# The 24 units of dilated attention between the dense matmuls of two runs, four steps a slot, a unit's weights turned one step behind its scores

## What is computed

```python
h = rms_norm(x, norm_w); proj = h @ w_in            # split into a_u, a_v, a_z, b_q, b_k, b_v, b_z, m_q, m_z, g
q = rms_norm(b_q per head, b_q_norm_w); k = rms_norm(b_k per head, b_k_norm_w); v = b_v    # 12 heads of 64
for gi, (window, dilation) in enumerate(((128, 1), (512, 4), (2048, 16))):                  # 4 heads each
    scores = q_block @ k_blocks.T / 8 + bias          # causal, window // dilation steps back
    m = max(scores); p = exp(scores - m); l = sum(p); o = p @ v / l; lse = m + log(l)
wts = softmax(stack(lses)); y_b = sum(wts * o) * silu(b_z)
# y_a: gelu(a_u), gelu(a_v), spatial gating, silu(a_z);  y_m: attention to 256 memory tokens, silu(m_z)
merged = sigmoid(g0) * (y_a @ proj_a) + sigmoid(g1) * (y_b @ proj_b) + sigmoid(g2) * (y_m @ proj_m)
x = x + merged @ w_out                                # second_block follows, untouched
```

## Time and profile before

| | us |
|---|---|
| median of 2 runs | 1762.23 (1761.26 to 1763.2) |
| span of the profiled execution | 1759.4 |
| PE busy / weight loads busy | 1726.5 / 1398.6 |
| DVE / ACT / POOL busy | 914.9 / 654.1 / 249.0 |
| the stretch of dilated attention alone (262.7 to 326.4) | 63.7 |
| PE / DVE / ACT busy in it | 60.2 / 53.6 / 56.0 |
| granted TensorE clock in it | 0.97 of full speed |

### The profile page before, as it was taken

How to read it: one execution, slowest core, us unless ns; L and a number is a source line. 1 busy time by engine, 2 the same in 40 slices (tenths; PEclk the granted TensorE clock), 3 DMA queues, 4 the chain that set the end, 5 groups by cost and what they waited for, 6 DMA issues and landing times.

```text
span 1759.4 us, 22322 instructions
## 1 busy us (share of the span) xinstructions
PE 1726.5 (98%) x8731; PEld 1398.6 (79%) x8731; DVE 914.9 (52%) x1528; ACT 654.1 (37%) x1225; POOL 249.0 (14%) x412
## 2 busy tenths in 40 slices
PE   7999999999999999999999999999999999999998
PEld 5788887778888888778888788888887777777786
DVE  5158868664336744763222322467242545657764
ACT  5234438611324432752112211233313363434731
POOL 3012210188801100000000000482000000000000
PEclk9999999999999999999999999999999999999999
DMA  4121110346232200311111221242713111001132
GB/s 145 52 76 47 37 37 2 118 144 192 85 123 72 61 25 13 94 30 49 54 42 52 66 63 31 96 144 79 156 31 99 42 31 37 25 25 48 40 130 107
DMA packets 148339, 122.93 MB, mean 70 GB/s; under 512 B 10555, under 2 KB 133898, under 8 KB 147594
## 3 DMA queue, kind: packets, MB, share of 16 engines
q1 hardware_dynamic: 148234, 121.49, 22.9%
HBM read 108.21 MB, written 13.26 MB: 69 GB/s over the span
## 4 chain that ended last, share of the span: by engine, by line
PE 56%; DVE 2%; ACT 1%; issue 1%; DVEq 0%; ACTq 0%
PE psum L93 30%; PE psum L278 10%; PE psum L81 7%; PE psum L2707 2%; PE psum L2738 2%; PE psum L2721 1%; PE psum L1720 1%; PE psum L945 0%; PE psum L931 0%; PE psum L2503 0%; PE psum L2524 0%; PE psum L920 0%; PE psum L2217 0%; DVE ya_low L1572 0%; PE psum L1481 0%
## 5 line engine op out<-in xcount | busy, mean ns | idle before, releaser
L93 PE MATMUL psum<-hT,w_parts 128*128 128x512 f32 x3360 | 796.4, 393 | 7.1 <-PEq L61 3.4
L93 PEld LDWEIGHTS psum<-hT,w_parts 128*128 128x128 f32 x3360 | 629.3, 189 | 144.7 <-issue 8.9
L221 DVE TENSOR_TENSOR w_parts<-w_raw,w_parts 128x1024 fp32r<-128x1024 f32 x88 | 111.7, 1270 | 364.9 <-ACT w_parts L210 364.9
L93 PE MATMUL psum<-h2T,w_parts 128*128 128x512 f32 x1248 | 297.1, 394 | 0.0
L93 PEld LDWEIGHTS psum<-h2T,w_parts 128*128 128x128 f32 x1248 | 230.8, 188 | 48.3 <-issue 1.7
L1514 ACT ACTIVATE gate<-psum,cols 128x512 f32<-128x512 f32 x48 | 33.1, 689 | 284.1 <-PE psum L81 284.0
L81 PE MATMUL psum<-y_high,wp_parts 128*128 128x512 f32 x384 | 128.8, 395 | 0.3 <-DVE ya_low L1572 0.3
L210 ACT CAST w_parts<-w_raw 128x1024 fp32r<-128x1024 f32 x88 | 91.6, 1041 | 24.7 <-DMA w_raw<-w_in 19.5
L81 PEld LDWEIGHTS psum<-y_high,wp_parts 128*128 128x128 f32 x384 | 72.0, 188 | 18.9 <-DVE ya_low L1572 1.6
L278 PE MATMUL psum<-w_parts,y_parts 128*128 128x512 f32 x360 | 82.6, 390 | 0.6 <-DVE w_parts L271 0.6
L403 DVE RECIPROCAL x<-x 128x512 f32<-128x512 f32 x24 | 80.2, 3341 | 0.0
(11 more groups left out here) (377 smaller groups left out, 2298.5 us busy)
## 6 DMA issues: line engine op xcount, KB each, us to landing
w_raw<-w_in SPq DMA_DIRECT2D x188, 256.0 KB, 3.4
middle_a<-ada_w SPq DMA_DIRECT2D x32, 384.0 KB, 3.7
w_raw<-w_out SPq DMA_DIRECT2D x16, 512.0 KB, 3.8
qkT<-x SPq DMA_DIRECT2D x8, 512.0 KB, 7.9
w_raw<-m_w_kv SPq DMA_DIRECT2D x16, 256.0 KB, 3.1
base<-x SPq DMA_DIRECT2D x8, 512.0 KB, 4.0
x_kept<-x_ring SPq DMA_DIRECT2D x8, 512.0 KB, 3.8
base<-x_kept SPq DMA_DIRECT2D x8, 512.0 KB, 3.6
```

What stands on the lines that cost most here:

```text
L93: last = pe.matmul(out, lhs(a, k), rhs(b, k), start=(n == 0), stop=(n == len(SLOT) - 1))
L221: dve.tensor_tensor(self.parts[:, u, LO, :, :], self.raw[:, :, :], self.parts[:, u, HI, :, :].bitcast(F32), ALU.subtract).then_inc(self.lo ...
```

## The change

In words: the 24 units are cut into 26 *bodies*. Body b does, on PE, scores of unit b, the turn of unit b-1 and the mix of unit b-2 (`lag=1`); on ACT the copy of unit b-1 and the exponentials of unit b; on DVE the store of unit b-3, the maxima of unit b and the copy of unit b-1. A slot has four places for a body, on PE behind 6, 12, 18 and 24 dense matmuls. Bodies 0 to 14 stand in slots 36 to 39 of the first run (body 0 at slot 36's second place), bodies 15 to 25 in slots 0 to 2 of the middle run. On ACT and DVE the first three places are written at the slot's start and the fourth at its end: on ACT behind the slot's eviction and the rounding of weights, on DVE behind the weights' low part and `vector_last`.

Dense matmuls keep two banks (0, 1) in these slots, so one score buffer is left (banks 2-3), one `pT`, and the weights lie in three places. The middle run's tile 0 is rounded in slot 37 (`ahead_high`, `ahead_low` at the last-but-one tile instead of at the run's end; this holds for the middle run's end too). Join starts two slots later (`FIRST = 3`) and spreads both pairs of a group in one slot (slots 5, 6, 7); Modulation starts in slot 4, the SSM loads in slot 3, MemNorm in slot 21, with its steps 3 slots apart and not 4. One more normal tile stands ahead of the memory's small tiles, and the last two of these follow each other.

```diff
@@ Dense.tensor
-            slot_part(pe, out, lhs, rhs, range(8))
+            slot_part(pe, out, lhs, rhs, range(6))
+            for work in self.beside:
+                work.tensor_body(pe, s, 0)
+            slot_part(pe, out, lhs, rhs, range(6, 8))
...
                 work.tensor_mid(pe, s)
+                work.tensor_body(pe, s, 1)
...
                 before.after(pe, self, s - 1)
+            for work in self.beside:
+                work.tensor_body(pe, s, 2)
             last = slot_part(pe, out, lhs, rhs, range(18, 24))
@@ Dense.scalar
+            for place in range(3):
+                for work in self.beside:
+                    work.scalar_body(act, s, place)
...
             if slot.last and slot.n + 2 < len(self.tiles):
                 w.split_high(act, slot.n // 2 + 1, slot.n % 2)
+            elif slot.last and slot.n + 2 == len(self.tiles) and self.ahead:
+                self.ahead.ahead_high(act)
             for work in self.beside:
                 work.scalar(act, s)
+                work.scalar_body(act, s, 3)
...
-        if self.ahead:
-            self.ahead.ahead_high(act)
@@ Dense.vector
+            for place in range(3):
+                for work in self.beside:
+                    work.vector_body(dve, s, place)
...
+            elif slot.last and slot.n + 2 == len(self.tiles) and self.ahead:
+                self.ahead.ahead_low(dve)
             self.tiles[slot.n].vector(dve, self, s)
             if s:
                 self.tiles[self.slots[s - 1].n].vector_last(dve, self, s - 1)
             for work in self.beside:
                 work.vector(dve, s)
+                work.vector_body(dve, s, 3)
@@ Attention.scores
             pe.wait_ge(self.maxed, u - before + 1)
-            pe.wait_ge(self.exped, u - before + 1)
+            if self.units[u - before]["bias"] is None:
+                pe.wait_ge(self.exped, u - before + 1)
@@ Attention.maxima
+        if u >= 2:
+            dve.wait_ge(self.exped, u - 1)
@@ DilatedAttention
-        super().__init__(core, stack, units, ident, p, pT, (0, 2), 4, (6, 7), lag=2)
+        super().__init__(core, stack, units, ident, p[0], pT, (2,), 4, (6, 7), lag=1)
+    def body_pe(self, pe, b):
+        lag = self.lag
+        if b < self.n:
...
+            self.scores(pe, b)
+        if 0 <= b - lag < self.n:
+            if b == lag:
+                pe.wait_ge(self.before.rooted, len(self.before.heads))
+            self.turn(pe, b - lag)
+        if b - lag - 1 >= 0:
...
+            self.mix(pe, b - lag - 1)
+    def body_act(self, act, b):
+        if 0 <= b - self.lag < self.n:
+            self.move_act(act, b - self.lag)
+        if b < self.n:
+            self.exps(act, b)
+    def body_dve(self, dve, b):
...
+        if 0 <= b - self.lag - 2:
+            self.store(dve, b - self.lag - 2)
+        if b < self.n:
+            self.maxima(dve, b)
+        if 0 <= b - self.lag < self.n:
+            self.move_dve(dve, b - self.lag)
@@ Join.tensor
-        if 2 <= s < 8:
-            g, pair = (s - 2) // 2, s % 2
+        if 2 <= s < 5:
+            g = s - 2
...
+            for pair in range(2):
+                if g:
+                    pe.wait_ge(self.used, 2 * g + pair - 1)
@@ first_block
+            last_slots = run.first_slot(len(values + queries + keys))
+            first_bodies = DilatedBodies(dilated, 0, 4 * last_slots + 1)
+            run.beside.append(first_bodies)
+            last_bodies = DilatedBodies(dilated, first_bodies.body(len(run.slots) - 1, 3) + 1, 0, after_last=True)
```

More of the change, by code:

```diff
@@ L517, in scalar @@
             work.scalar_start(act)
-        if self.heads:
+        if self.heads and not self.same_at:
             act.copy(self.same, self.same_from).then_inc(self.same_made, 1)
@@ L890, in __init__, with place @@
                 "stored"))
+    def place(self, u):
+        return self.p[u % self.ring]
     def S_(self, u):
```

239 lines of the change are left out of this document (127 added, 112 removed).

## The result

| | before | after |
|---|---|---|
| median, first measurement | 1762.23 (2 runs) | 1788.4 (2 runs) |
| ratio with its 95% interval | | 1.0154 [1.0138, 1.0171] |
| median, second measurement | 1762.16 (10 runs) | 1788.12 (4 runs, 1785.7 to 1790.2) |
| ratio with its 95% interval | | 1.0143 [1.0128, 1.0159] |
| span of the profiled execution | 1759.4 | 1786.7 |

A forecast was written before the change was run, and what follows sets the result against it. PE, busy 1726.5 of 1759.4 us, was taken as the bound. Fill -5.6, switches +6.0, waits +26.3, clock +3.2, Join and rest -1.8 gave +28.1: span 1787.5, median 1790 us, range 1766 to 1804.

The forecast's parts named there:

- Switches: Going from dense matmuls to a unit and back on PE costs 0.23 us, 26 bodies: +6.0 us.
- The stretch's fill and drain go: Filling and draining of the dedicated dilated attention stretch, lowered clock included, disappears: -5.6 us.
- Waits: New PE waits for a unit's scores or turn between dense matmuls, four kinds: +26.3 us.
- (a): Slot 36: the heads' reciprocals on DVE stand ahead of the first units' maxima, delaying scores and turns: 7.4 us.
- (b): Slot 37, the runs' border, middle run's slot 1: maxima wait behind a tile's rounding and low part: 12.3 us.
- (c): Slots 38, 39 and middle run's slot 0: Exp's table load after Silu's delays the turn: 4.4 us.
- (d): Copy of one unit waits for the mix before it through one `pT`, in seven wide bodies: 2.2 us.
- The clock: Two falls of the clock behind PE's waits, 1.65 us each: +3.2 us.
- Join and the rest: Join's spreading matmuls -1.35, middle run's end -0.8, small tiles' wait 1.0; together -1.8 us.
- Not slower: Rival: DVE's and ACT's order does not bind, dense matmuls cover the chain; 1754 to 1765 us, chance 0.09.
- Half hidden: Rival: PE's waits absorb the switches, and DVE and ACT run ahead; 1765 to 1777 us, chance 0.13.
- The waits stack: Rival: each delayed step delays those behind it, with four clock falls; over 1797.5 us, chance 0.18.

The follow-up runs named there:

- all_off: Changed kernel with one head tile's reciprocal cut to 64 columns, fourth body ahead of rounding and low part, Copy for Silu at eight pieces, lag of two: 1765.3 us.
- order3: Changed kernel with the fourth body's exponentials and maxima ahead of the weights' rounding and low part in a tile's last slots: 1786.5 us.
- all_but_order: Changed kernel with reciprocal cut to 64 columns, Copy for Silu and lag of two, but its own order on ACT and DVE: 1765.1 us.
- best: Kernel before with units 0 and 1 started in slots 37 and 38, Join's two pairs in one slot, next run's first weights rounded earlier: 1757.8 us.
- after_again: The changed kernel once more with no edit: 1788.12 us.
- recip_cut: Changed kernel with the reciprocal of one head tile's roots taking 64 columns instead of 512 in slots 34 and 35: 1784.8 us.
- order_tables: Changed kernel with the fourth body ahead of rounding and low part, and Copy for Silu in the gates and the middle run's first two tiles: 1782.7 us.
- no_tables: Changed kernel with Copy instead of Silu for the first run's gates and the middle run's first two tiles: 1778.6 us.

## Why the prediction was right, and where it was not

**Switches: right.** Six dense matmuls between two bodies of after take 1.59 us where nothing waits (335.47 to 337.06 on PE's timeline), against 1.36 for six of a long row: 0.23, the value of the earlier trace rows. all_off agrees with the sum. The Trainium skill (TensorEngine Tiling (Array Packing), Key Properties) has TensorE drain at a change of the tiling mode; the trace agrees in so far as a visit costs that 0.23 us.

**The stretch's fill and drain go: in line with the runs, and it is all there was to win.** With every new cause off, the changed kernel still stands 4.1 us over the kernel before: the switches cost what the fill gave, and some waits remain.

**Waits: right in their places, too large in sum.** Forecast were 26.3 of waits, 3.2 of clock and -5.6 of fill, 23.9 together; the rows give 16.5 and at most 8.2, 24.7. From start to start, with the time from a release to the matmul, the units of after lose 21.2 us by waits, 5 less than forecast.

- (a) The reciprocals: 7.4 forecast; 3.82, 0.34, 0.41 and 0.99 at slot 36 are 5.6, or 5.9 from start to start. Taken away alone it gave 3.3, put back alone it cost 5.5. The cause is shown, and with it that ACT's roots and table load are the next to be waited for.
- (b) Maxima behind a tile's weights: 12.3 forecast at three places; there the rows have 9.5 (2.39, 0.97; 1.01, 1.39; 2.74, 0.96), or 9.9 from start to start. Places and chain were right, and the rows of DVE at 278.32 show it. What did not hold is that the order of rounding, low part and maxima is the cause by itself: turning it round should bring back the 7.1 us at slot 37 and slot 1, and neither order3 (waits 19.6 of 19.7) nor all_but_order (1765.1 against 1765.3) shows any worth of it. The unit is late at a slot's end because a table load, eviction, rounding and low part, or else eviction, copy and two table loads, stand between a slot's last matmul and a turn one body later. The two chains are of nearly one length.
- (c) Tables: 4.4 forecast as waits of their own; 1.03, 1.04 and 1.56 at 304.06, 322.07 and 342.75 are 3.6, one behind each of the slots named. The size was right, but it is not what the loads cost: taking 14 of them away gave 9.6, for Silu's load also delays the rounding and so the maxima of (b), and with shorter waits four of five lengths of low clock went. The Trainium skill (ScalarE: Activation LUTs, What ACT_TABLE_LOAD costs) adds a drain to a load; in order3's rows the exponential follows the load of 280.30 within 0.02 us of its end, and here as in the earlier trace rows no drain shows (there the first exponential starts at 264.72).
- (d) One `pT`: 2.2 forecast, the four waits of 0.25 and 0.26 before turns, 1.0 together. Not tried by itself, since a second buffer has no room.

**The clock: mis-sized, and the step that failed.** Two falls of 1.65 were forecast for 3.2. The units of after have five lengths of 3.4 us low; where PE works in them it loses 6.7 us from start to start (1.2, 1.6, 1.5 and, behind the double one, 2.4), and at the middle run's end the fall doubled (+1.2): 7.9. The prediction took the number of falls from the one in the stretch of before; the changed kernel waits 3.8 us, 2.4 and 1.0, 1.0 and 1.4, 2.7 and 1.0, and has a fall behind each of the four. That the total came out nearly exact is luck: waits 5 us too large and clock 4.7 us too small cancel.

**Join and the rest: in line, not measured alone.** 27.3 at the end, 25.2 at L1837, 26.9 behind the small tiles, 26.1 at the middle run's end: the wait of the small tiles was 1.42 (1.0 forecast), the gain at the end 0.8 as forecast. Behind slot 3 the shift grows by no more than 2.1 us. The -1.35 for Join's matmuls was not taken apart in the changed kernel; in best, with the weights rounded earlier, it is part of 3.9.

**The rivals.** "Not slower" turned on the reciprocals and the order on DVE; all_off, which takes the reciprocals, the order, the tables and the short lag away, lands at 1765.3, the upper edge of it (1754 to 1765); the order alone decided nothing. "Half hidden" did not happen: switches and waits add. "The waits stack" needed four falls and half of the waits more; there were four low stretches, one of them double, and fewer waits than forecast. ACT and DVE are only 63% and 55% busy from 243 to 365 us, and in most bodies between the slots' ends PE waits 0.26 us at most.

## What to carry to other kernels

Before units are put between dense matmuls, ask what the stretch they come from wastes: here 5.6 us, a price that 26 changes of the matmuls' form eat by themselves. Then follow the unit through the slot's end, not the order of two instructions: eviction, rounding, table loads and reciprocals make a chain, and with a turn one step behind its scores each link counts; removing one link of two equally long chains buys nothing. No change of table inside the mixed slots (9.6 us) and a lag of two (5.0) gave more than the reordering (1.6). And where PE is 97% busy, a wait costs its length and, in this kernel, often some 1.5 us of clock behind it.

## What the runs showed of the hardware

The time at the low clock came in portions of about 3.4 us (now and then 6.8): 3.4, 3.4, 3.4 and 6.8 in the units of after, the same in after_again, and none in all_off. A portion cost 1.2 to 1.7 us where PE was busy. In after, falls stand behind waits of 3.8, 2.4 and 2.7 us and behind two of 1.01 and 1.39 us that follow each other, in the kernel before behind 1.82; none behind the single waits of 1.03, 1.04 and 1.56 at 304.06, 322.07 and 342.75. The same waits do not always bring a fall: the pair of 1.02 and 1.39 at the border has none in recip_cut and order3, and behind single waits of 2.65 (order3, at 363.8) and 2.60 (order_tables, at 355.6) the clock stays up. Behind the 3.8 it fell in every kernel that has it. In order_tables fewer waits than in no_tables went with more low time, so of a change worth two or three microseconds the sum of waits tells less than it seems. Executions of one kernel differ by as much as a few such portions: best took 1752.9 to 1760.8 us at mean clocks of 0.998 to 0.994, and by estimate 0.004 x 1757 x 2 / 2 = 7 us of the spread of 7.9 are the clock.
